# Loads of the routed experts' rows in a hybrid decoder step: a token's rows sorted by expert, the two lowest fetched before the last passes have scattered

## The reference, cut to what matters

```
eidx, gw = route(x2, w_router, router_bias)          # 6 experts of each token, by falling score
ffn = swiglu(x2, shared) + routed_experts(x2, eidx, gw, w_e_gate, w_e_up, w_e_down)
#     routed_experts: y[t] = sum over the 6 of gw[t, j] * swiglu(x2[t], expert eidx[t, j])
ple = sigmoid(h @ w_ple_gate) * (p @ w_ple_proj)
h = layer_norm(DN_ALPHA * h + ffn + ple, ln2_g, ln2_b)
```

## Time and profile before

| | us |
|---|---|
| median of 3 runs | 1266.23 |
| lowest and highest | 1265.12, 1267.54 |
| profiled execution | 1267.28 |
| its span, first to last instruction | 1265.4 |
| TensorE busy | 1227.0 (97%) |
| VectorE busy | 497.9 (39%) |
| ScalarE busy | 306.3 (24%) |
| GpSimd busy | 159.8 (13%) |

### The profile page before, as it was taken

How to read it: one execution, slowest core, us unless ns; L and a number is a source line. 1 busy time by engine, 2 the same in 40 slices (tenths; PEclk the granted TensorE clock), 3 DMA queues, 4 the chain that set the end, 5 groups by cost and what they waited for, 6 DMA issues and landing times.

```text
span 1265.4 us, 23325 instructions
## 1 busy us (share of the span) xinstructions
PE 1227.0 (97%) x8776; PEld 974.0 (77%) x8777; DVE 497.9 (39%) x1103; ACT 306.3 (24%) x560; POOL 159.8 (13%) x228
## 2 busy tenths in 40 slices
PE   7999999999999999999899999999999999999977
PEld 7988879999999999998899666556555566666643
DVE  4456574423453433566886112112112221111137
ACT  4344453322221222316012111111111111111121
POOL 0200000000000000004336121111111121211100
PEclk9999999999999999999999999999999999999999
DMA  9312122322223232606337999999999999999986
GB/s 279 103 37 67 34 68 51 80 71 79 89 68 100 67 109 76 211 21 208 141 115 305 420 419 419 421 421 419 420 421 419 420 421 418 420 421 421 421 351 264
DMA packets 98656, 307.31 MB, mean 243 GB/s; under 512 B 11244, under 2 KB 62404, under 8 KB 72840
## 3 DMA queue, kind: packets, MB, share of 16 engines
q1 hardware_dynamic: 85332, 275.20, 56.2%
q0 software_dynamic: 12304, 28.60, 5.8%
q10 hardware_dynamic: 948, 2.50, 0.6%
HBM read 294.45 MB, written 26.94 MB: 254 GB/s over the span
## 4 chain that ended last, share of the span: by engine, by line
PE 55%; DMA 37%; DVE 5%; issue 1%; DVEq 1%; ACT 0%; SPq 0%; POOL 0%; ACTq 0%; POOLq 0%
DMA w_exp<-in_w_e_down_dram 35%; PE proj L1051 32%; PE proj L1243 4%; PE proj L1384 3%; PE att L1454 2%; PE proj L1473 2%; PE att L1165 2%; PE att L1127 1%; DMA fold<-expert_rows 1%; PE att L1252 1%; PE proj L1338 1%; PE att L1178 1%; PE proj L1368 1%; PE proj L1077 1%; DVE res L2124 1%
## 5 line engine op out<-in xcount | busy, mean ns | idle before, releaser
L1454 PE MATMUL att<-w_exp,xt 128*64 128x256 f32 x2560 | 286.3, 380 | 2.7 <-DMA w_exp<-in_w_e_up_dram 2.1
L1454 PEld LDWEIGHTS att<-w_exp,xt 128*64 128x64 f32 x2560 | 207.6, 137 | 90.2 <-issue 27.5
L1051 PE MATMUL proj<-h_hi,w_hi 128*128 128x288 f32 x768 | 171.1, 304 | 0.0
L1051 PE MATMUL proj<-h_hi,w_lo 128*128 128x288 f32 x768 | 164.2, 295 | 0.0
L1051 PE MATMUL proj<-h_lo,w_hi 128*128 128x288 f32 x768 | 164.0, 295 | 0.0
L1473 PE MATMUL proj<-w_exp,ht_e 128*64 128x512 f32 x640 | 146.1, 597 | 9.6 <-DMA w_exp<-in_w_e_down_dram 4.9
L1051 PEld LDWEIGHTS proj<-h_hi,w_hi 128*128 128x128 f32 x768 | 122.0, 188 | 16.2 <-issue 15.2
L1051 PEld LDWEIGHTS proj<-h_lo,w_hi 128*128 128x128 f32 x768 | 123.5, 188 | 0.0
L1051 PEld LDWEIGHTS proj<-h_hi,w_lo 128*128 128x128 f32 x768 | 123.4, 188 | 0.0
L468 DVE TENSOR_TENSOR w_lo<-w_raw,w_hi 128x2048 fp32r<-128x2048 f32 x33 | 75.6, 2291 | 91.9 <-ACT w_hi L458 86.8
L1473 PEld LDWEIGHTS proj<-w_exp,ht_e 128*64 128x64 f32 x640 | 50.4, 136 | 77.7 <-issue 76.0
(11 more groups left out here) (384 smaller groups left out, 1810.8 us busy)
## 6 DMA issues: line engine op xcount, KB each, us to landing
w_exp<-in_w_e_gate_dram SPq DMA_DIRECT2D x64, 1024.0 KB, 16.9
w_exp<-in_w_e_up_dram SPq DMA_DIRECT2D x64, 1024.0 KB, 17.0
w_exp<-in_w_e_down_dram SPq DMA_DIRECT2D x64, 1024.0 KB, 17.1
w_raw<-in_w_in_dram SPq DMA_DIRECT2D x21, 1024.0 KB
part<-expert_rows SPq DMA_DIRECT2D x8, 1536.0 KB, 21.2
w_raw<-in_w_in_dram SPq DMA_DIRECT2D x8, 512.0 KB
w_raw<-in_w_attn_out_dram SPq DMA_DIRECT2D x8, 512.0 KB
w_raw<-in_w_conv_out_dram SPq DMA_DIRECT2D x4, 1024.0 KB
```

The costliest lines, as they stand in the source:

```text
L1051: last = nc.tensor.matmul(proj[:, 2 * i + a, 0:HALF], lhs, x[:, c, a * HALF:(a + 1) * HALF], start=(c == 0 and n == 0), stop=(c == KC - 1 ...
L1454: last = nc.tensor.matmul(att[e * SLOT:(e + 1) * SLOT, m, 0:FF], xt[:, c, e * SLOT:(e + 1) * SLOT], weights[e][:, c, :], start=(c == 0), s ...
```

## The change

- A token's six experts are sorted by their number, highest first, before `hot` is built: the indices as floats (-2 in what is unused), five MAX8 operations, and the comparison against their result. So place 0 of a prompt token holds its highest expert and place 5 its lowest. Prompt tokens now use places 0 to 5 of their 8; sample tokens keep 0, 1, 2, 4, 5, 6.
- A prompt tile is read as `low[t]` (places 4 and 5, one load of 1 MB) and `high[t]` (places 0 to 3, two loads of 1 MB) instead of two halves of 1.5 MB.
- SP no longer waits for the last scatter first. When pair 29's products are done and its scatter has landed (`pair_landed`), it issues low 0 and 1; when pair 30's products are done, low 2; then it waits for `all_out` and issues high 0, fold, high 1, low 3, high 2, and after pair 31's products high 3.
- TensorE adds three rows of every prompt tile: 4, 5 and 0 of tiles 0, 2 and 3, and 0, 1 and 2 of tile 1 (`ON_PE`); the last of them comes behind the product for the last pass. Its tail begins when the last transposed tokens are read, not when the last pass's result is.
- VectorE adds rows 1, 2 and 3 of tiles 0, 2 and 3. Of tile 1 it adds 4 and 5 before and after `y_lo`, and 3 in its turn.

```diff
-N_ON_PE = (3, 3, 4, 4)
+ON_PE = ((4, 5, 0), (0, 1, 2), (4, 5, 0), (4, 5, 0))
+LOW = 4
...
+    place_of = np.where(tok < SEQ, np.arange(6)[None, None], np.array([0, 1, 2, 4, 5, 6])[None, None])
+    val = np.where(tok < T, tok * 8 + place_of + 8, 0).astype(np.float32).reshape(P, -1)
...
-            sp.wait_ge(all_out, 1)
...
+            def pair_landed(p):
+
+                done = sp.value_load(cum_pass[0:1, p:p + 1], min_val=1, max_val=MAXPASS - 1)
+                sp.wait_ge(scattered, done * 16 + 16)
+                past(nc.sync, 4)
...
             pair_done(NPE - 3)
-            for h in range(2):
-                load_rows(0, h)
+            pair_landed(NPE - 3)
+            load_low(0)
+            load_low(1)
+            pair_done(NPE - 2)
+            load_low(2)
+            sp.wait_ge(all_out, 1)
+            load_high(0)
             rows = rows_d[SEQ * 8:T * 8, :].rearrange("(q i) n -> q i n", i=4)
             sp.dma_start(fold[:, :, :], rows[:, 0:3, :]).then_inc(part_in[NT - 1], 16)
-            load_rows(1, 0)
-            pair_done(NPE - 2)
-            load_rows(1, 1)
-            for h in range(2):
-                load_rows(2, h)
-            load_rows(3, 0)
+            load_high(1)
+            load_low(3)
+            load_high(2)
             pair_done(NPE - 1)
-            load_rows(3, 1)
+            load_high(3)
...
             k = pe.snap(count, min_val=0, max_val=MAXPASS - 2)
-            pe.wait_ge(y_a, k + 1)
-            pe.wait_ge(y_dv, k + 1)
+            pe.wait_ge(xt_a, k + 1)
+            pe.wait_ge(xt_d, k + 1)
...
+                    rows = ON_PE[t]
+                    for j in rows[:-1]:
+                        row_sum(s, t, j, j == rows[0], False)
+                    last_product(s, t, False)
+                    row_sum(s, t, rows[-1], False, True).then_inc(part_sum, 1)
...
-            nc.vector.tensor_copy(eidx_f[:, :, :], eidx[:, :, 0:TOPK])
-            dve.drain()
-            nc.vector.memset(eidx_f[NS:P, NT - 1, :], -1.0)
-            dve.drain()
+            nc.vector.tensor_copy(eidx_f[:, 0:NT - 1, 0:TOPK], eidx[:, 0:NT - 1, 0:TOPK])
+            nc.vector.tensor_copy(eidx_f[0:NS, NT - 1, 0:TOPK], eidx[0:NS, NT - 1, 0:TOPK])
+            dve.drain()
+            for t in range(NT):
+                nc.vector.max(ebest[:, t, :], eidx_f[:, t, :])
             dve.drain()
...
+            add_low(1, 4)
             dve.wait_ge(y_hi_ready, 1)
             dve.drain()
             nc.vector.tensor_tensor(y_lo[:, :], ysb[:, 1, :], y_hi[:, :].bitcast(F32), ALU.subtract).then_inc(y_lo_ready, 1)
+            add_low(1, 5)
...
-                for j in range(N_ON_PE[t], TOPK):
-                    nc.vector.tensor_tensor(r, r, part_row(t, j), ALU.add)
-                    dve.drain()
+                for j in range(LOW):
+                    if j not in ON_PE[t]:
+                        nc.vector.tensor_tensor(r, r, part_row(t, j), ALU.add)
+                        dve.drain()
```

More of the change, by code:

```diff
@@ L344, in decoder_step @@
         rows_d = nc.dram_tensor("expert_rows", [T * 8, D], F32)
[L345 to L348, removed]
+        o_low = [o + 4 * n * D for o, n in ((o_w2, 0), (o_w2, 2), (o_w0, 0), (o_w0, 2))]
+        o_high = [o + 4 * n * D for o, n in ((o_w2, 4), (o_w0, 4), (o_w0, 8), (o_w1, 0))]
+        low = [at(f"low{t}", [P, TOPK - LOW, D], F32, o_low[t]) for t in range(NT - 1)]
+        high = [at(f"high{t}", [P, LOW, D], F32, o_high[t]) for t in range(NT - 1)]
+        fold = at("fold", [P, TOPK // 2, D], F32, o_w2 + 4 * 8 * D)
         slot_hot = at("slot_hot", [P, T], F32R, o_x)
@@ L359, in part_row @@
             c0 = (half or 0) * 512
-            return part[t][j // 3][:, j % 3, c0:c0 + (D if half is None else 512)]
+            return (high[t][:, j, :] if j < LOW else low[t][:, j - LOW, :])[:, c0:c0 + (D if half is None else 512)]
         def sum_banks(n):
@@ L1512, in _, with last_product, row_sum @@
                     pair(it * 3 + (N_UNROLLED + i), RING[(N_UNROLLED + i) % 3])
+            def last_product(s, t, stop):
+                w = ntok(t)
+                pe.wait_ge(y_lo_ready, 1)
+                for half in range(2):
+                    for n, y in enumerate((y_hi, y_lo)):
+                        last = nc.tensor.matmul(sum_banks(s)[0:w, half, :], slot_hot[:, t * P:t * P + w],
+                                                y[:, half * 512:(half + 1) * 512], start=False, stop=(stop and n == 1))
+                return last
+            def row_sum(s, t, j, start, stop):
+                if j >= LOW:
+                    pe.wait_ge(low_in[t], low_base[t] + 16)
+                elif j < 2:
+                    pe.wait_ge(part_in[t], 16)
+                else:
+                    pe.wait_ge(tile_in[t], 32)
+                for half in range(2):
+                    last = nc.tensor.matmul(sum_banks(s)[:, half, :], ident[:, :], part_row(t, j, half), start=start, stop=stop)
+                return last
             k = pe.snap(count, min_val=0, max_val=MAXPASS - 2)
-            pe.wait_ge(y_a, k + 1)
-            pe.wait_ge(y_dv, k + 1)
+            pe.wait_ge(xt_a, k + 1)
+            pe.wait_ge(xt_d, k + 1)
             past(nc.tensor, 1)
@@ L1527, in _ @@
                         for j in range(TOPK // 2):
-                            nc.tensor.matmul(out[:, half, :], fold_id[:, :], fold[:, j, half * 512:(half + 1) * 512],
+                            nc.tensor.matmul(sum_banks(s)[0:NS, half, :], fold_id[:, :], fold[:, j, half * 512:(half + 1) * 512],
                                              start=(j == 0), stop=False)
+                    last_product(s, t, True).then_inc(part_sum, 1)
                 else:
[L1531 to L1542, removed]
-                    for half in range(2):
-                        last = nc.tensor.matmul(out[:, half, :], ident[:, :], part_row(t, TOPK // 2 + j, half),
-                                                start=False, stop=(j == more - 1))
-                last.then_inc(part_sum, 1)
+                    rows = ON_PE[t]
[3 more added lines that the diff above has]
+                    row_sum(s, t, rows[-1], False, True).then_inc(part_sum, 1)
         @block.vector
@@ L1842, in _ @@
             nc.vector.memset(scores[NS:P, NT - 1, :], 0.0)
+            nc.vector.memset(eidx_f[:, :, :], -2.0)
             dve.wait_ge(sc_ready, 1)
```

26 lines of the change are left out of this document (16 added, 10 removed).

## The result

| | us |
|---|---|
| before, median of 11 runs | 1265.43 (1263.62 to 1267.54) |
| changed, median of 11 runs | 1269.36 (1267.96 to 1271.01) |
| ratio, 95% interval | 1.0026 [1.0018, 1.0035] |
| the changed kernel once more, on another chip | 1269.11, ratio 1.0029 [1.0018, 1.0040] |
| profiled execution, span: before | 1267.28, 1265.4 |

The change costs 3 to 4 us. The two profiles differ by only 1.6, because the profiled execution of before was among the slowest of its runs (later ones of the same kernel: median 1265.49 of 29). So the profiles are compared stage by stage, from fixed points.

What follows compares the result with a forecast made beforehand. The end was taken as bound by the fold rows' landing, TensorE's fold product and VectorE's work per tile. Terms +2.2 + 0.8 + 0.4 + 0.4 = +3.8 us on the profiled 1267.28 gave 1271.1, median 1270.0, range 1267.5 to 1272.

Steps and rivals of the forecast that it cites:

- The fold lands later: Load queue at the end: the sample tokens' rows land 2.2 us later, at 1229.6; bounds -1.7 to +5.0.
- Bytes ahead: Load queue: 6.82 MB instead of 4.72 land up to and including the fold, costing 5.0 us at 421 GB/s.
- The start saved: Load queue: low loads queued before the last scatter save the 2.8 us by which the stream began behind the last weights.
- Rival 1: Load queue, 1207 to 1227: DMA engines even out, fold lands 0.7 us sooner, total +0.1, 1266.3; chance 0.25.
- The clock around the fold product: TensorE at the fold: longer idling ahead of the product prolongs its low clock, +0.8 us; bounds 0 to +3.2.
- the loss grows from 1.9 to about 2.7: Fold product on TensorE: microseconds lost to the low clock, as idle time rises from 2.31 to about 4.5 us.
- Rivals 2 and 3: Fold product: full clock with the fold 1.7 us sooner, 1263.4, chance 0.10; all at low clock, 1272.4, chance 0.13.
- VectorE behind the fold: Tile sums at the end: seven adds in both versions, but VectorE waits for TensorE's tile 1, +0.4 us.
- The early adds: Tile 1's two low rows, added while VectorE waits anyway: no cost; 2.6 us without that cover.
- The routing: VectorE's sort, drain and small extra steps in the routing, not hidden: +0.4 us; bounds 0 to +0.6.
- The marks set for the next profile: Tail signs: fold landing near 1229.6, plus 0.4 for the routing; VectorE's first sum for the fold near 1239.

Runs made afterwards that it cites:

- e1: The kernel before plus only the change's sort of each token's experts and its wide comparison; 1265.33 us, ratio 0.9998 to before.
- e3: The changed kernel with the wait for the last scatter put in front of all loads, their order kept; 1272.19 us, ratio 1.0059 to before.
- e4: The changed kernel with only low 0 issued early, tile 1's two low adds moved to just before the fold's sum; 1264.63 us, ratio 0.9994 to before.
- e2: The changed kernel with low 2 issued behind the fold instead of ahead of it; 1266.61 us, ratio 1.0006 to before.
- e9: The changed kernel with tile 0's two low rows multiplied once more on TensorE ahead of its fold wait; 1266.98 us, ratio 1.0008 to before.
- e5: The changed kernel with VectorE's adds of tile 1's low rows moved behind the fold's scaling, before tile 1's sum; 1270.78 us, ratio 1.0045 to before.
- e8: The changed kernel with the sort's five MAX8 and the drain behind them done nine times; 1272.23 us, ratio 1.0053 to before.
- e10: The changed kernel with 24 unused products on TensorE ahead of its wait for the first routing table; 1268.49 us, ratio 1.0022 to before.

## Why the prediction was right

Forecast 1270.0, measured 1269.36 and 1269.11; +3.8, measured 3.9 by the medians and 3.3 by the ratio (0.0026 of 1265.4). The steps, and where errors met:

- **The sum held better than its parts.** Two profiles can stand for the loads and products of before, and they split the same cost differently. From e1's tail to the changed one: fold 1.22 later, product 1.70 longer, rest 0.60, in all 3.52; with 0.51 for the sort 4.0. From before's: 1.87, 0, 0.59, and 0.51, in all 3.0. The medians say 3.9. So a forecast of 2.2 for the fold and 0.8 for the clock may have been too high in the first and too low in the second by about as much; that the sum came out within 0.1 of the medians is in part luck.

- **The fold lands later: +2.2 forecast, +1.87 measured against before, +1.22 against e1** (14.18 and 14.83 to 16.05). Both halves were seen alone. Bytes ahead: 5.0 forecast, 5.03 from W or 4.9 from the first issue (e3 against before). The start saved: 2.8 forecast, 3.16 (changed against e3). Rival 1, that the engines even out and the fold lands 0.7 sooner, is not what happened, though the mean DMA share rose to 1.02. With one low load ahead the engines were 0.73 busy from 1207 to 1211 and 0.58 to 1213 (e4), and still 2.54 of gain came. So the first megabyte ahead bought nearly all, and the next two cost 2.35 and 2.06 each (e4 to e2 to changed). The Trainium skill, "DMA: Bandwidth & Descriptors", section "Anatomy of one DMA — SWDGE (gpsimd) path", has a fixed cost of about 2.0 us for a DMA that GpSimd issues; these loads are SyncE's, and the start that they saved is 3.16. What makes up the 3.16 (the spread of the sixteen engines was the guess) no run here takes apart.
- **The clock around the fold product: +0.8 forecast, 0 in the profiled pair.** This is the mis-sized term. The step "the loss grows from 1.9 to about 2.7" failed in the profile: 7.06 in both, behind 2.31 and behind 4.20 us, a loss of 1.7 each against the 5.36 that full clock gives (the forecast took 5.2). Behind 4.2 us the product took 7.06, 7.06, 7.06, 8.00 and 7.96, a mean loss of 2.1 against 5.36, and e9 gives 2.1 by the medians. For before there are two samples only, 7.06 in the fold product and 7.08 in tile 0's rows with 5.36 behind them. Against e1 the difference is 1.70. What the average execution of before loses there stays open; it may well be a microsecond less than the changed kernel's. Rivals 2 and 3 (full clock; the whole product at half clock) both fell.
- **The Trainium skill's "TensorE: Matmul & The Clock Gate", section "HAM oscillation",** has the next group start slow after a wait for DMA. All eight profiles with 2.3 to 4.2 us of waiting ahead of the fold agree in so far as the product took 6.78 to 8.00, and the six with 1.44 or less had 5.36 or 5.37; but in none was it slow to its end, which would be 10.3. e9, which cut the wait to 0.76 us by filling it, had the full clock.
- **VectorE behind the fold: +0.4 forecast, +0.59 measured** (from the fold's sum to the last sum 22.16 before, 22.75 after). The wait for tile 1's sum is 0.30; the rest is 0.1 in each of the three intervals (8.34 and 8.33 with three adds, where the row used had 8.24, and 6.08 less the 0.30 with one, where 5.67 was worked out). Nearly all of this 0.1 is a longer gap in front of a tile's first add, 1.42 to 1.43 us from the start of the scaling (line 2185) to the start of the add, instead of 1.35 to 1.36; the changed kernel waits there for two semaphores instead of one, and that this is the cause is not tested. The early adds are covered as argued: low1 landed at 1217.2 (forecast 1218.2), and without the cover they cost 2.22 (e5; 2.6 forecast, less the wait).
- **The routing: +0.4 forecast, +0.51 measured** from the MAX8 ahead of the sort to `hs_f` (13.73 against before's 13.22; the same 0.5 to the first table, 32.29 against 31.79). The clock times differ by only 0.28 (631.98 for 631.70), because before's profile came to the sort 0.22 later. e8 shows that such a delay is paid nearly in full.
- **What was missed:** before's profile lost more in the routing than any other one here. Its first table product took 2.14 and the gate products behind it 4.63, against 1.84 and 3.76 after. The difference, 1.17 us, was paid in full: with the 0.22 that lay ahead of the sort, and less the 0.51 of the sort, it makes the 0.89 by which the changed kernel's first weights go out sooner. The changed kernel's own loss there is nearly free (0.24 against e3 and e4, 0.33 against e10). This, and before's low clock at the fold, hide some 2 us of the change in the profiled pair. The marks set for the next profile (fold at 1230.0, first sum at 1239) were therefore 1.6 and 2.4 too late, while the median was right: taking off the 1.05 by which before's profile lay above its median corrected in the sum what the parts did not show.

Idle DMA time ahead of the fold was worth having, but only for the bytes that stood ahead of it already. The change spent it on three megabytes, two of which the fold did not need.

## What to carry to other kernels

Issue early only what already stood ahead of the critical transfer in the queue; every megabyte more cost 2.1 to 2.5 us here, most or all of its transfer time, even when the mean DMA share was low before. Measure stages from an event inside each profile, since one profile against another can hide 2 us of a change of 3.9; and ask what releases the transfer in question, since an event that doesn't release it is a ruler with an error of its own (0.65 us here). A wait of TensorE that the path goes through can be filled with products that compute nothing, but only up to the landing: twice the filler lost all that the right length gained, and where another engine is close behind, as in the routing, it gained 0.3 us and the medians hardly moved.

## What was unexpected of the hardware

- The low clock does not follow from the length of the wait alone. Behind the same 3.41 us in the routing, e3 and e4 kept 1.00 from 630 to 642 (first table product 1.15), while in the nine others with this wait it fell to 0.50 to 0.60 in at least one stretch of 2 us between 632 and 636; behind 4.2 us ahead of the fold, the product took 7.06 or 8.0. And as little as 2.31 us (before) and 2.45 us (e1) of waiting was followed by 0.50, while 1.44 us and less ahead of the fold product never was.
- With three low loads queued the mean DMA share was 1.02 from 1207 to 1213, with one it was 0.68, and one already brought the fold 2.54 sooner than before. The saving of the early issue (3.16 us) was more than the 2.8 worked out from landings.
- VectorE's work for one tile takes 8.33 or 8.24 us with the same instructions; the gap in front of the first add, behind two semaphores or one, is 1.43 or 1.36, and whether the second semaphore makes the difference was not tested.
